# The convolution of the last up block divided among the first three residuals of the down pairs

## The reference

```python
def conv_ffn(h, w_up, conv_w, conv_b, w_down):
    S = h.shape[1]
    u = h @ w_up
    u_p = jnp.pad(u, ((0, 0), (CONV_WIDTH - 1, 0), (0, 0)))
    c = conv_b
    for j in range(CONV_WIDTH):
        c = c + conv_w[j] * u_p[:, j:j + S]
    gate, val = jnp.split(c, 2, axis=-1)
    return (jax.nn.silu(gate) * val) @ w_down
```

## Time and profile before

| | us |
|---|---|
| three runs | 3564.49, 3568.81, 3571.47 |
| median | 3568.81 |
| profiled execution | 3572.91 |
| its span | 3570.9 |
| TensorE busy in the span | 3407.0 |
| VectorE busy in the span | 1723.9 |

### The profile page before, as it was taken

One profiled execution on the slowest core, in us unless ns is written; L12 is line 12 of the kernel. 1 busy time (PEld: TensorE's weight loads), 2 busy tenths in 40 slices (PEclk: granted clock), 3 DMA queues, 4 the chain that ended last, 5 costly groups with the idle time before them and its releaser, 6 DMA issues.

```text
span 3570.9 us, 31399 instructions
## 1 busy us (share of the span) xinstructions
PE 3407.0 (95%) x12290; PEld 1798.3 (50%) x12290; DVE 1723.9 (48%) x3094; ACT 990.9 (28%) x2079; POOL 205.2 (6%) x203
## 2 busy tenths in 40 slices
PE   7999999999989999999999899899999999999997
PEld 3556554565456544544565565664444444444443
DVE  2056282144146281551465554654336656556556
ACT  4244111102244111022477845631111000000001
POOL 0000000020000000100000000000110011201121
PEclk9999999999999999999999999899999999999998
DMA  5100122130000001111001101211001101111012
GB/s 209 56 7 13 58 75 76 47 115 30 30 12 13 29 27 44 45 49 42 36 24 36 36 20 46 76 46 50 25 24 36 47 30 53 39 38 53 30 42 71
DMA packets 52209, 163.73 MB, mean 46 GB/s; under 512 B 5552, under 2 KB 9904, under 8 KB 51389
## 3 DMA queue, kind: packets, MB, share of 16 engines
q1 hardware_dynamic: 47194, 145.82, 11.8%
q10 hardware_dynamic: 4868, 15.91, 1.3%
HBM read 157.46 MB, written 11.32 MB: 47 GB/s over the span
## 4 chain that ended last, share of the span: by engine, by line
PE 85%; DVE 8%; ACT 4%; issue 1%; SPq 1%; DMA 0%; POOL 0%; DVEq 0%; ACTq 0%; POOLq 0%
PE ps L605 26%; PE ps L635 14%; PE ps L1285 14%; PE ps L1047 5%; PE ps L763 4%; PE ps L1058 2%; PE ps L786 2%; PE ps L942 2%; PE ps L775 2%; PE ps L1070 2%; ACT sb L1821 1%; PE ps L1125 1%; PE ps L1136 1%; DVE sb L2081 1%; PE ps L1032 1%
## 5 line engine op out<-in xcount | busy, mean ns | idle before, releaser
L605 PE MATMUL ps<-sb 128*128 128x512 f32 (+1 forms) x2448 | 963.4, 554 | 14.0 <-ACT sb L1624 6.7
L1344 ACT ACTIVATE sb<-ps 128x512 f32<-128x512 f32 (+10 forms) x729 | 362.9, 514 | 1620.5 <-PE ps L605 465.6
L605 PEld LDWEIGHTS ps<-sb 128*128 128x128 f32 x2448 | 466.5, 191 | 504.9 <-issue 480.1
L635 PE MATMUL ps<-sb 128*128 128x512 f32 x1232 | 540.5, 599 | 16.9 <-DVE sb L2665 14.5
L1285 PE MATMUL ps<-sb 128*128 128x512 f32 x1232 | 531.9, 594 | 3.7 <-DVE sb L2709 3.7
L635 PEld LDWEIGHTS ps<-sb 128*128 128x128 f32 x1232 | 235.3, 192 | 318.0 <-issue 289.5
L1285 PEld LDWEIGHTS ps<-sb 128*128 128x128 f32 x1232 | 234.4, 191 | 300.2 <-issue 293.1
L1047 PE MATMUL ps<-sb 128*128 128x512 f32 x512 | 231.3, 599 | 0.0
L763 PE MATMUL ps<-sb 96*128 96x512 f32 (+1 forms) x400 | 157.4, 529 | 5.2 <-ACT sb L1533 4.5
L2217 DVE SCALAR_TENSOR_TENSOR sb<-sb 128x1310 f32<-128x1310 f32 (+1 forms) x120 | 161.7, 1430 | 0.0
L1821 ACT ACTIVATE sb<-sb 128x384 int8<-128x384 f32 (+4 forms) x160 | 152.2, 953 | 2.4 <-DVE sb L2376 0.7
(11 more groups left out here) (264 smaller groups left out, 3412.4 us busy)
## 6 DMA issues: line engine op xcount, KB each, us to landing
sb<-in_w_in SPq DMA_DIRECT2D x73, 512.0 KB, 3.3
sb<-in_w_ada SPq DMA_DIRECT2D x48, 512.0 KB, 4.4
sb<-in_w_up SPq DMA_DIRECT2D x44, 512.0 KB, 3.4
sb<-in_w_down SPq DMA_DIRECT2D x40, 256.0 KB, 2.8
sb<-in_w_out SPq DMA_DIRECT2D x16, 512.0 KB, 3.7
sb<-in_w_mkv SPq DMA_DIRECT2D x16, 512.0 KB, 3.2
rows_dram<-vec_dram ACTq DMA_DIRECT2D x1, 6906.0 KB
sb<-rows_dram ACTq DMA_DIRECT2D x6, 1024.0 KB, 5.3
```

Of the source, the lines that this page charges most:

```text
L605: ins = mm(ps[:, 0:tn], w[:, k, :], src(k, t0, tn), start=(k == 0), stop=(k == nk - 1))
L635: ins = mm(ps[:, 0:512], stationary(k), moving(k), start=(first and k == 0), stop=(k == h - 1), skip_group_check=not first)
L1344: return act(out, in_, func, scale=scale)
```

## The change

In VectorE's program of a down stage, the convolution of the group's last up block (`behind`) is divided. The three gate instructions stay behind the residual of pair 0. The three value instructions go behind the residual of pair 1, the product behind the residual of pair 2. `conv` gets an argument that says which sides it does.

```diff
             for p in range(4):
                 seven_residual(DOWNS[g], p, ("x4", g), add)
-                if p == 0:
-                    conv(behind)
+                if p < 2:
+                    conv(behind, (p,))
+                elif p == 2:
                     product(behind)
...
-        def conv(f):
+        def conv(f, sides=(0, 1)):
 
             g = f // SLOT_F
             if g >= 2 and f % SLOT_F == 0:
                 e.wait_ge(*at((DOWNS[g - 2], "seven", 3, "p3")))
-            for s in range(2):
+            for s in sides:
```

## The result

The changed kernel takes 3546.54 us in the median of four runs (3546.18 to 3550.03) against 3567.59 us for the kernel before (four runs, 3564.49 to 3571.47): ratio 0.9945, 95% interval 0.9932 to 0.9958, 21 us less. The forecast was 3549 us, the range 3543 to 3557. The profiled execution of after took 3546.45 us with a span of 3544.5 us, 26.4 us less than the span of before.

What follows compares the result with a forecast made beforehand. TensorE bounds the kernel, busy 95% of the span, stopping for VectorE's backlog in five down stages. Savings of 16.2 (stops) and 6.1 us (clock) make 22.3: 3572.91 to 3550.6 profiled, 3549 taken for the median, range 3543 to 3557.

Steps and rivals of the forecast that it cites:

- What is won: Five down stages: 262.66 us before against 240.35 ideal at 0.4292 us a record, so 22.3 us to win.
- The two parts: Down stages: 16.2 us from stops and restarts, five times 3.25; 6.1 from clock falls in first, fourth and fifth.
- Gate behind pair 0, Silu: Down stage: gate convolution stays at 14.54 to 17.91 us, ScalarE's waiting Silu runs at the same time; no cost.
- Residual of pair 1: VectorE, right after the gate: `c22 c` done by 19.2 us, wanted at 22.3, 3.1 to spare; the stop goes.
- Value behind pair 1: VectorE, after pair 1's residual: takes 3.4 to 4.65 us from 26.55, ending at 29.9 to 31.2, taken as 30.
- Residual of pair 2: VectorE, after the value, the tightest place: 1.8 to 3.1 us to spare at `c22 c`, 1.2 to 3.1 at `c22 d`.
- Product behind pair 2: VectorE, after pair 2's residual at 38.57 us: takes 1.5, ends at 40.1; pair 3's `c22 c` keeps 2.5 to spare.
- Rival A: Down stages: the stop goes, the clock's share does not; only 16.2 us won, 3556.7 or 3552.6 us; chance 0.12.
- Rival B: The wait moves to p4 or p3 of pair 2; about 3561 us if half lost, 3572.9 if all; chance 0.05.
- Rivals C and D: C: GpSimdE's sums for pair 3 starve, 3588 us, chance 0.02. D: order not as written, 3572.9 us, chance 0.01.
- The median: Whole kernel: profiled run stands 4.1 us above median; if clock falls explain it 3550.6 us, otherwise 3546.5; taken 3549.

Runs made afterwards that it cites:

- e1: Against the kernel before: convolution left whole behind pair 0, only the product moved behind pair 2; 3553.66 us, median of seven.
- joins first: Against the changed kernel: in the first up group and next block, joins of blocks 1 and 4 go ahead of the next block's weight sums; 3544.67 us.
- e6: Against the changed kernel: three more VectorE instructions of 128x1024 ahead of the value convolution behind pair 1; 3547.31 us, median of five.
- e3: Against the changed kernel: gate, value and product all behind the residual of pair 1; 3565.02 us, median of ten.
- e7: Against the changed kernel: five more VectorE instructions of 128x1024 ahead of the value convolution behind pair 1; 3562.15 us, median of ten.
- e2: Against the changed kernel: product early, behind pair 1 with the value instead of behind pair 2; gate stays behind pair 0; 3544.55 us, median of four.
- e5: The changed kernel again, nothing altered, run beside the kernels with added work; 3550.05 us, median of five.
- e4: Against the changed kernel: convolution divided only in the first, third and fifth down stage, whole behind pair 0 in the others; 3557.48 us, median of ten.

## Why the prediction was right, point by point

- **What is won.** Forecast 22.3 us in the five stages, measured 22.3. The step that carried it was to take the ideal length from the kernel's own up group (0.4292 us a record) and not to add up idle time, which would have given 14.5.
- **The two parts.** The 3.25 us of a stage without a fall are gone in every stage of after, and in e1 a stop 1.67 us shorter makes the stage 1.65 us shorter than 51.31. The clock's 6.1 us belong to the stops: in 28 stages without one (after, the change again, product early, joins first, three more, and three of the divided kernel) there was no fall; behind the stage stops of 1.23 us 0 of 5 had one, of 1.97 (with 0.57 ahead) 2 of 5, of 2.17 1 of 5, of 2.9 7 of 12, of 5.46 5 of 5. (The 0.40 us of e6 do not show as a stop in the timeline.) Rival A did not come about.
- **Gate behind pair 0, Silu.** At no cost, as said; e3 shows what it would have cost elsewhere (0.57 us a stage).
- **Residual of pair 1.** `c22 c` at 19.2 us as forecast, 3.1 to spare. The two adds from SBUF took 1.85 us; I had taken 2.3, the upper price.
- **Value behind pair 1.** Forecast at 26.55 to 30, measured 26.6 to 30.0. GpSimdE's sums began at 29.5 (forecast 29.4).
- **Residual of pair 2.** Forecast 1.2 to 3.1 to spare, measured 2.6 at `c22 d`. Its two adds from SBUF took 1.76 us beside the sums, between the 1.2 and 2.3 counted. Rival B did not happen, and e7 shows where it begins: 4.2 us more make a stop of 2.17 there, 2.5 us more hardly any.
- **Product behind pair 2.** Right in time (38.6), but unnecessary (e2). The sum could not have said so for certain: it left 1.2 to 3.1 us at `c22 d` of pair 2 for a product of 1.5. Behind pair 1 the product took that much, beside GpSimdE, and 0.9 us stayed to spare.
- **Rivals C and D.** GpSimdE was never starved: its first sums for pair 3 took 1.11 and 0.73 us beside VectorE. And the order came out as written: the timeline has the three pieces where the code puts them.
- **The median.** The mis-sized term. I offered two readings of the 4.1 us by which before's profiled execution stood above its median: falls in the down stages that the median run did not have, or nothing to do with the stages. The second led to 3546.5, I took 3549, and 3546.54 was measured. The traces lean to the second too: 4.0 us of before's profiled execution lie ahead of the stages and are absent in after, and before once more has its falls in the stages again (263.96 us for the five). But no run at before's median was profiled, so this is not shown, and that 3546.5 was met to a tenth is luck: five more runs of the same kernel had a median of 3550.05. The saving is steadier than the time: 21.05 us between the medians of the result and 21.00 between those of the runs beside e5, against 19.8 taken and 22.3 in the stages of the traces.

## What to carry to other kernels

When one engine stops for another's backlog, ask how much of that backlog stands between two of its deadlines, and cut it there; the order of the rest is free as long as each piece is smaller than the slack at the next deadline, and e1 to e3 show that the amount decides and not the place. Take the ideal length of a stage from an undisturbed stretch of the same kernel and compare whole stages: restarts and the lower clock behind a stop are then in the sum, here 7.8 us on top of 14.5 of idle. Look also at what stands behind the moved step on other engines' queues (the Silu ahead of a copy), since that decides which piece should stay.

## What was unexpected in the hardware

One kernel's executions differ by up to 21 us (before: 3558.04 to 3578.89 over the runs beside the experiments) with the same instructions, and part of it can be placed: falls of TensorE's clock behind its waits, each 1.4 to 2.9 us. The same 2.60 us wait in the first up group had a fall in 2 of 11 profiled executions that have it, the 2.9 us stops of the down stages in 7 of 12. The Trainium skill ("TensorE: Matmul & The Clock Gate", Part 1) says that the number of matmuls at the lower clock differs from run to run; the traces agree, and they add that a stop of 1.23 us had none in five and one of 5.46 us had one each time.

The count by length hides a second pattern. Of the 22 stage stops of 2.0 to 2.9 us (before twice, e3, e4, e7), those of the first stage had a fall in 4 of 4, the fourth in 4 of 5, the fifth in 2 of 4, the second in 0 of 5 and the third in 0 of 4. In the same five places the 1.23 us stop had none and the 5.46 us stop had one each, in one execution of each kernel, so length seems to count, but it is not all that counts. Nor does a fall need a stop of 2 us: behind three waits of 0.3 to 0.7 us and one of 0.61 ahead of L1224, the same eight records took 5.37 us in 7 of the 12 profiled executions and 3.67 in the other 5. What decides between them no run here shows.
